# One layer pair of a hybrid diffusion trunk: reordered scan chunks, a group norm with gathered variances, output projections as block products

## The reference

```python
# RWKV, per head of 64 and direction d
S = S * w_t + sa * b_t + v_t * k_t ;  y_t = S r_t          # scan
y  = y_fwd + y_bwd + bonus terms                           # 512 features
mu, var = mean and variance over the 64 of a head
y  = (y - mu) * rsqrt(var + 64e-5) * ln_g + ln_b
y  = y * (sigmoid(gd) @ g_up)
out = concat([attention, y]) @ w_out                       # 1024 x 1024
x   = x + gate * out                                       # gate per feature and group

# layer 1
out = u @ w_out + b_out                                    # 1024 x 1024
x   = x + gate * out
```

## Time and profile before

| what | us |
|---|---|
| runs shown | 5159.09, 5168.80, 5169.05 (median 5168.8) |
| the profiled execution's own time | 5160.96 |
| its span, first to last instruction | 5159.2 |
| PE busy in the span | 4524.0 (88%) |
| DVE, ACT, POOL busy | 2522.4, 1017.9, 394.1 |
| latent scan, 15 chunks with `ahead` (1341 to 1807) | 466.0 |
| group norm (1837.2 to 1923.5) | 86.3 |
| first output projection (1923.5 to 2067.3) | 143.8 |
| second output projection (4011.7 to 4157.3) | 145.6 |

### The profile page before, as it was taken

The page is one execution under the profiler, slowest core; times in us unless marked ns, Lnnn a source line. Parts: engine busy times, 40 slices in busy tenths (PEclk is TensorE's granted clock), DMA queues, the critical chain, the costliest instruction groups (busy, mean ns, idle before and its releaser), DMA issues. The chain is left out here.

```text
span 5159.2 us, 73362 instructions
## 1 busy us (share of the span) xinstructions
PE 4524.0 (88%) x30480; PEld 3509.3 (68%) x30480; DVE 2522.4 (49%) x3679; ACT 1017.9 (20%) x1892; POOL 394.1 (8%) x385
## 2 busy tenths in 40 slices
PE   5989789954799949899999989969997889999997
PEld 3656378843788835677777767747776457777775
DVE  6755367777688851422223333447776242222332
ACT  2000056652344410200000022221121020000002
POOL 0000100000000000121110011100000011211000
PEclk7999989976899979999999999979998999999998
DMA  4354100010000001111114212220010311111520
GB/s 148 122 202 146 50 15 7 5 69 1 5 0 0 0 32 40 71 39 41 41 56 125 60 68 85 79 102 31 16 37 28 113 63 41 41 41 33 145 71 37
DMA packets 253992, 297.55 MB, mean 58 GB/s; under 512 B 18306, under 2 KB 209131, under 8 KB 252686
## 3 DMA queue, kind: packets, MB, share of 16 engines
q1 hardware_dynamic: 243486, 250.40, 15.0%
q10 hardware_dynamic: 7648, 30.81, 1.5%
q0 software_dynamic: 2704, 14.16, 0.8%
HBM read 240.68 MB, written 51.51 MB: 57 GB/s over the span
## 5 line engine op out<-in xcount | busy, mean ns | idle before, releaser
L896 PE MATMUL acc<-arena 128*128 128x288 f32 x4928 | 1205.5, 408 | 38.1 <-ACT arena L336 24.2
L896 PEld LDWEIGHTS acc<-arena 128*128 128x128 f32 x4928 | 941.6, 191 | 302.4 <-issue 38.3
L443 PE MATMUL acc<-arena 128*128 128x384 f32 x1824 | 606.5, 495 | 65.9 <-DMA arena<-in_ab_w_out 25.8
L702 PE MATMUL acc<-arena 128*128 128x288 f32 x2464 | 597.8, 406 | 0.0
L443 PEld LDWEIGHTS acc<-arena 128*128 128x128 f32 x1824 | 351.1, 194 | 309.3 <-issue 78.9
L702 PEld LDWEIGHTS acc<-arena 128*128 128x128 f32 x2464 | 468.2, 190 | 129.4
L2192 PE MATMUL acc<-arena 128*128 128x288 f32 x1344 | 333.2, 412 | 16.3 <-ACT arena L336 11.7
L2192 PEld LDWEIGHTS acc<-arena 128*128 128x128 f32 x1344 | 259.1, 193 | 90.6 <-issue 16.8
L2544 PE MATMUL acc<-arena 128*128 128x256 f32 x1280 | 280.9, 380 | 5.2 <-DVE arena L2716 3.4
L2544 PEld LDWEIGHTS acc<-arena 128*128 128x128 f32 x1280 | 241.9, 190 | 40.6 <-DVE arena L2716 6.2
L1332 DVE TENSOR_REDUCE arena<-acc 128x1 f32<-128x1280 f32 (+1 forms) x144 | 195.5, 1358 | 101.7 <-PE acc L1258 94.4
(11 more groups left out here) (345 smaller groups left out, 5908.9 us busy)
## 6 DMA issues: line engine op xcount, KB each, us to landing
arena<-in_ffn_w SPq DMA_DIRECT2D x44, 1024.0 KB, 5.3
arena<-in_ffn_w SPq DMA_DIRECT2D x64, 704.0 KB, 6.5
arena<-in_ada_w SPq DMA_DIRECT2D x20, 2048.0 KB, 10.3
scratch_x_d<-arena SPq DMA_DIRECT2D x3, 4608.0 KB, 17.2
scratch_z_d<-arena SPq DMA_DIRECT2D x24, 576.0 KB, 2.8
arena<-scratch_z_d SPq DMA_DIRECT2D x12, 1152.0 KB, 6.4
arena<-in_hy_w_in SPq DMA_DIRECT2D x12, 1024.0 KB, 5.1
arena<-in_ab_w_in SPq DMA_DIRECT2D x22, 512.0 KB, 4.2
```

Of the source, the lines that this page charges most:

```text
L443: last = pe.matmul(k.bank(tc, TC), slab[j][:, kt, :], src(kt)[:, tc * TC:(tc + 1) * TC], start=(kt == 0), stop=(kt == n_k - 1))
L702: mm = pe.matmul(acc(m, j)[:, s, :], slot[left[m][j]][:, kt, :], right[m][:, kt, s * TS:(s + 1) * TS], start=(kt == 0), stop=(kt == KH - 1))
L896: last = pe.matmul(acc(w, m)[:, s, :], left[:, kt, :], right[:, kt, s * TS:(s + 1) * TS], start=(kt == 0), stop=(kt == 3))
```

## The change

**Scan.** The two additions of the bonus into `ya` move from ahead of the masks to behind the masks of the large Gram matrices. `ark1` is split: its products come ahead of the additions into `ya` at the chunk's end, its copies of the decay stay at the end.

**Group norm.** PE sums and gates all four tiles first (the gate goes into the output tile by ACT). The squares of tile t and column block c (128 tokens) are multiplied by a 72-column window of a constant whose ones select rows, so that all 8 heads x 9 column blocks of variances gather in one bank of 72 x 128. One root and one reciprocal of that size follow. PE then spreads each row back over 64 partitions by products with a 72 x 4608 matrix, which POOL makes from the identity, and DVE multiplies. In the same stage SP issues the loads of the first two weight slabs (256 columns each) and of the eight `x` tiles for the projection that follows; the semaphore reset moves ahead of the stage.

**Both projections** go over from `stage_gemm` to a new `stage_projection`: four pairs of output tiles, seven products each. In the second nothing is loaded ahead: SP loads a slab, four of the input tiles and a slab, ACT the other four input tiles, and POOL, once these eight are there, issues the eight loads of `x` before its first weight sums. There ACT adds gate times bias onto `x`. The constant block grows from 1096 to 1238 columns.

```diff
             def step(i, ahead):
                 dve.wait_ge(pe_s.sem, pe_s.here(i, "bonus", not ahead))
                 dve.tensor_tensor(tmp, u64(pb(3)), vc, ALU.mult).then_inc(dve_s.sem, 1)
-                for d in range(2):
-                    dve.drain()
-                    dve.tensor_tensor(ya[:, :, cols(i, d)], ya[:, :, cols(i, d)], tmp[:, 4 * d:4 * d + 4, :], ALU.add)
...
                     last.then_inc(dve_s.sem, 1)
+                for d in range(2):
+                    dve.tensor_tensor(ya[:, :, cols(i, d)], ya[:, :, cols(i, d)], tmp[:, 4 * d:4 * d + 4, :], ALU.add)
+                    dve.drain()
                 for n in lvl:
...
                 dve.wait_ge(pe_s.sem, pe_s.here(i, "y", not ahead))
+                if ahead:
+                    ark1(i, 1)
...
                 if ahead:
-                    ark1(i, 1).then_inc(dve_s.sem, 1)
+                    dve.drain()
+                    decay_ends().then_inc(dve_s.sem, 1)
...
+            for p in range(2):
+                sp.dma_start(slab[p], wview[:, :, 256 * p:256 * p + 256]).then_inc(slab_in[p], 16)
+            for m in range(KT):
+                load_x_tile(k, sp, scratch, m, x_in)
...
+            def variances(t):
+                pe.wait_ge(squared, t + 1)
+                for c in range(9):
+                    last = pe.matmul(k.bank(6)[0:72, 0:128], head_window(k, t, c), sq[:, t, c * 128:(c + 1) * 128],
+                                     start=(t == 0 and c == 0), stop=(t == 3 and c == 8))
...
+                if t:
+                    variances(t - 1)
+            variances(3)
+            pe.wait_ge(inverted, 1)
+            pe.wait_ge(rows_made, 1)
+            for t in range(4):
...
+                if t >= 2:
+                    pe.wait_ge(normed, t - 1)
+                for c in range(9):
+                    last = pe.matmul(k.psum[:, 1536 * (t % 2) + c * 128:1536 * (t % 2) + (c + 1) * 128], rows[:, 64 * (8 * c + 2 * t):64 * (8 * c + 2 * t) + 128], rstd, start=True, stop=True)
...
+            dve.wait_ge(rooted, 1)
+            dve.reciprocal(rstd, rstd).then_inc(inverted, 1)
+            for t in range(4):
+                dve.wait_ge(spread, t + 1)
+                dve.tensor_tensor(ya[:, t, :], k.psum[:, 1536 * (t % 2):1536 * (t % 2) + T], ya[:, t, :], ALU.mult).then_inc(normed, 1)
+                if t:
+                    dve.wait_ge(scaled, t)
+                    dve.tensor_tensor(out[:, t - 1, :], out[:, t - 1, :], ya[:, t - 1, :], ALU.mult)
...
+def stage_projection(k, tag, src, layer, scratch, weights, loaded, bias=None, src_rows=None):
...
+            if not loaded:
+                pool.wait_ge(src_in[0], 64)
+                pool.wait_ge(src_in[1], 64)
+                for m in range(KT):
+                    load_x_tile(k, pool, scratch, m, x_in)
+            for p in range(pairs):
...
+                pool.tensor_tensor(s1, a21, a22, ALU.add).then_inc(step_done, 1)
+                pool.tensor_tensor(s3, a11, a21, ALU.subtract)
...
+                pool.tensor_tensor(s2, s1, a11, ALU.subtract).then_inc(step_done, 1)
...
+                pool.tensor_tensor(s4, a12, s2, ALU.subtract).then_inc(wsum_ready, 1)
...
+                product(p, "M1", a11, h11)
+                if p == 0 and not loaded:
+                    pe.wait_ge(src_in[1], 64)
+                product(p, "M2", a12, h21)
+                pe.wait_ge(wsum_ready, p + 1)
+                if p == 0:
+                    pe.wait_ge(sums_ready, 2)
+                product(p, "M6", s2, t2)
+                product(p, "M5", s1, t1)
+                if p == 0:
+                    pe.wait_ge(sums_ready, 4)
+                product(p, "M7", s3, t3)
+                product(p, "M3", s4, h22)
+                product(p, "M4", a22, t4)
```

More of the change, by code:

```diff
@@ L1995, in _, with head_window, head_rows, spread_head_rows @@
                 dve.tensor_copy(st[:, 0:8, :], u64(pb(7))).then_inc(fin_copied, 1)
[L1998 removed]
+def head_window(k, t, c):
+    o, w = CCOL["heads"]
+    at = CST + o + 70 - (8 * c + 2 * t)
+    return k.arena[:, at:at + 72]
+def head_rows(k, at):
+    return k.at(at, 72 * 64)[0:72, :]
+def spread_head_rows(k, pool, rows, made):
+    pool.tensor_copy(rows.rearrange("p (n o) -> p n o", o=64),
+                     k.ident[0:72, 0:72].rearrange("p (n o) -> p n o", o=1).broadcast_to([72, 72, 64])).then_inc(made, 1)
+def stage_rwkv_post(k, A, scratch, weights):
     nc = k.nc
@@ L2003, in stage_rwkv_post @@
     gup = k.at(Z1, 512)
-    sq, root = k.tiles(Z1 + 1024, 2, T), k.tiles(Z1 + 1024 + 2 * T, 2, T)
+    sq = k.tiles(Z1 + 512, 4, T)
+    rstd = k.at(Z1 + 512 + 4 * T, 128)[0:72, :]
     eps = k.at(SM0 + 1, 1)
+    wview, slab, slab_in, x_in = weights
     S = lambda n: k.sem(f"gn_{n}")
-    gup_in, summed, centred, squared, var_ready, rooted, normed, gate_ready, done = (S(n) for n in (
-        "gup_in", "summed", "centred", "squared", "var", "root", "normed", "gate", "done"))
-    eps_set, scaled = S("eps"), S("scaled")
+    gup_in, gated, gate_kept, summed, centred, squared, var_ready, rooted, inverted, spread, normed, scaled = (S(n) for n in (
+        "gup_in", "gate", "gate_kept", "summed", "centred", "squared", "var", "root", "inverse", "spread", "normed", "scaled"))
+    eps_set, rows_made = S("eps"), S("head_rows")
+    rows = head_rows(k, Z1 + 640 + 4 * T)
     with nc.Block() as block:
@@ L2023, in _ @@
                 last.then_inc(summed, 1)
-                pe.wait_ge(squared, t + 1)
                 if t:
[L2026 to L2030, removed]
+                    pe.wait_ge(gate_kept, t)
                 for tc in range(3):
                     last = pe.matmul(k.bank(3 + tc, TC), gup[:, t * 128:(t + 1) * 128], rs[:, 13, tc * TC:(tc + 1) * TC], start=True, stop=True)
-                last.then_inc(gate_ready, 1)
+                last.then_inc(gated, 1)
@@ L2035, in _, with keep_gate @@
         @block.scalar
         def _(act):
+            def keep_gate(t):
+                act.wait_ge(gated, t + 1)
+                for tc in range(3):
+                    last = act.activation(out[:, t, tc * TC:(tc + 1) * TC], k.bank(3 + tc, TC), ACT.Copy)
+                last.then_inc(gate_kept, 1)
             act.wait_ge(eps_set, 1)
             for t in range(4):
+                keep_gate(t)
                 act.wait_ge(centred, t + 1)
-                act.activation(sq[:, t % 2, :], ya[:, t, :], ACT.Square).then_inc(squared, 1)
@@ L2041, in _ @@
[L2041 to L2044, removed]
+                act.activation(sq[:, t, :], ya[:, t, :], ACT.Square).then_inc(squared, 1)
+            act.wait_ge(var_ready, 4)
+            act.activation(rstd, k.bank(6)[0:72, 0:128], ACT.Sqrt, bias=eps[0:72, :], scale=1.0 / C).then_inc(rooted, 1)
@@ new lines, in _, with prefetch_projection, load_x_tile @@
+            dve.wait_ge(scaled, 4)
+            dve.tensor_tensor(out[:, 3, :], out[:, 3, :], ya[:, 3, :], ALU.mult)
+def prefetch_projection(k, tag, A_w, slab_at):
+    wview = A_w.rearrange("(k p) n -> p k n", p=128)
+    slab = [k.tiles(slab_at + 2048 * j, KT, 256) for j in range(2)]
+    slab_in = [k.sem(f"{tag}_slab_in{j}") for j in range(2)]
+    x_in = [k.sem(f"{tag}_x_in{m}") for m in range(KT)]
+    return wview, slab, slab_in, x_in
+def load_x_tile(k, eng, scratch, m, x_in):
+    eng.dma_start(k.X[:, m, :], scratch["x_d"][:, m * T:(m + 1) * T]).then_inc(x_in[m], 16)
@@ L2085, with stage_mixer_out @@
+def stage_mixer_out(k, A, scratch, weights):
+    stage_projection(k, "mix", k.tiles(OA0, 8, T), 0, scratch, weights, True)
 QUARTER = NL // 4
```

171 lines of the change are left out of this document (155 added, 16 removed).

## The result

The changed kernel took 5074.0 us (median of four runs, 5072.3 to 5082.1), the kernel before 5166.7 beside it: a ratio of 0.983, 95% interval 0.981 to 0.984 (the two medians alone give 0.982). Measured again later it was 5067.5 and 0.980 (0.979 to 0.982). The forecast was 5069.

A forecast was written before the change was run, and what follows sets the result against it. Bounds taken: PE in the scan, one chain per tile in the norm, PE after load waits in both projections. 17.6 + 39.9 + 27.3 + 10.1 − 0.2 = 94.7 off 5160.96 gave 5066.3, put at 5069, range 5057 to 5083.

The forecast's parts named there:

- the wait for the masks: Scan: PE's first level waits for DVE's masks, 22.5 us over 14 chunks; it would start 1.49 earlier per chunk.
- the copy is late next: Scan: PE's second level then waits 0.4 us for DVE's first copy, so 1.1 is won per chunk, not 1.49.
- two terms of 16 x 1.1: Scan: 16 chunks with `ahead` (15 latent, 1 context) each win 1.1 us, 17.6 in all.
- `ark1` at nothing: Scan: `ark1` stays on the same engine in the same chunk; its 0.7 us delays only a later product, gaining nothing.
- The rival's ground: Scan: DVE is the busier partner after the masks, so a later copy takes back the gain, 5087; chance 0.14.
- the chain as drawn: Group norm: sums and gates, variances, one root and reciprocal, spreading, DVE multiplications in sequence, 46.4 us against 86.3.
- the early loads take the wait for them away: First projection: loads issued in the norm arrive before it ends, so the next stage's wait for loads goes whole.
- the 12.8 to 15.3: First projection: when POOL's four sums end if a port lock alternates them with DVE's; stage up to 2.3 us longer.
- The rival that POOL's loads cannot be issued beside DVE: Second projection: loads of `x` wait for DVE's sums; gain at most 5 us, nothing with slow sums: 5079; chance 0.10.
- The bound of −1: Second projection: the smallest gain allowed for, 1 us, if POOL is slowed throughout.
- The marks: Signs named ahead, including as wrong: clock below 1.00 mid-projection, or a stage untouched by the change moving over 5 us.
- The rival of a slower kernel through the clock: Both projections: block products fed by waits leave PE at half clock, 5286 us with all at half; chance 0.03.

The follow-up runs named there:

- experiment 2: Changed kernel with only `ark1` put back whole at the chunk's end, the moved bonus additions staying: 5071.8 us.
- experiments 3 and 4: Changed kernel, first projection's loads issued in its own stage, not the norm: 5075.5 us; that projection also back to plain products with its own loads: 5099.8 us.
- experiment 6: Changed kernel with ACT instead of POOL issuing the eight loads of `x` in the second projection: 5075.7 us.
- experiment 10: The changed kernel profiled once more, unedited: end of attention at 1127.1 us instead of 1144.6, from there to the last instruction 3932.4.

## Why the prediction was right

**The scan** was right by its steps: the wait for the masks goes, the copy is late next. That the total came so close, 18.0 for 17.6, is partly luck, because two terms of 16 x 1.1 were off in opposite ways. A chunk gains 1.35, not 1.1, since the additions and the drain take 1.18 in their new place (1515.93 to 1517.11) where 1.49 was put down, and PE is only 0.2 late for the copy and not 0.4. And 14 chunks gain it, not 16: the first chunk of each group never had the wait. `ark1` at nothing holds (experiment 2). The rival's ground was misread: over this stretch has PE busy for 423 us and DVE for 373, so DVE is not the busier of the two.

**The norm** took 44.9 (first instruction to the next stage's first) where 46.4 was forecast, with the chain as drawn. POOL's copy, put at 11.4 from the additions of the earlier trace rows, took 4.03; it was covered either way. The reciprocal was 0.95 for an estimate of 0.82.

**The first projection** took 115.2 where 116.5 was forecast. Its weak step is the sentence that the early loads take the wait for them away. It goes, but experiments 3 and 4 show that most of it would go without them: about 10 of the 15 us because the slab no longer shares with one large load of `x`, while the early issue itself is worth 3.4. The size was right, the reason mostly not. POOL's sums were ready at 11.5 for an estimate of 13: POOL and DVE started together, POOL's first sum took 1.26 and three were slowed to some 3.4. The Trainium skill, SBUF — State Buffer, section "SBUF: two separate sides", describes the shared ports as a lock held for a whole instruction. The trace agrees in kind (three POOL sums of 3.29 to 3.58 among DVE sums of 3.33 to 3.66), while the 12.8 to 15.3 worked out from it were too long: from the second POOL sum on it is 3.25 to 3.55 us from one start to the next, less than 1.27 + 2.56.

**The second projection** won 11.9 for 10.1. The first product came at 11.9 (forecast 14), the third at 29.2 (30), and the first two products took 9.69 (10.8), so PE's wait was 7.6 and not 5. The rival that POOL's loads cannot be issued beside DVE fell: eight took 4.21, 0.53 each, with a DVE sum of 2.56 running. But POOL's queue was a real price: about 9.5 us, which experiment 6 took back. The bound of −1 does not follow from the forecast's own terms: with the sums at 36, 36 + 3.1 + 100.7 + 1.75 gives 141.6, that is −4.

**The marks.** One that I had named as proof of error came: a stage that the change does not touch moved by over 5 us. Without experiment 10 it would have passed for a cost of the change. The rival of a slower kernel through the clock fell: 0.98 and 0.92 in the two projections.

## What to carry to other kernels

Before paying for an early load, see what the late one shares the DMA with: issuing the slab that is needed first ahead of `x`, in one queue and in smaller loads, went with a gain of about 10 us, three times what starting everything a stage ahead gave. An engine that both issues loads and computes delays its computing by the wait ahead of the issues; give the issues to one with nothing behind them. And compare stage by stage from a common instruction: 79 us between the two profiled executions and 97 behind the end of attention were the same change.

## What was unexpected of the hardware

For the same instructions of the attention, PE busy for 30 of 30 us, the mean granted clock was anywhere from 0.50 to 1.00 from one execution to the next, and the attention's end moved by up to 20 us (1125.8 to 1145.6), more than most single parts of this change. Behind the same pause of 1.44 us in the norm the granted clock fell to 0.50 within the spreading in one profile of ten (14.76 us for 8.30, experiment 6). Idle products up to 1.15 us ahead of a stage kept its clock: 108.88 us instead of 110.73 for the same 448 instructions.
